# The gather of the next expert and the last transposes set between the slabs of the down product, and each scatter behind the next expert's first feature block

## The reference

```python
def moe_swiglu(h, router, w_gate, w_up, w_down):
    ...
    for e in range(N_EXPERTS):                      # 8 experts, D_FF_EXPERT = 2816
        y = y + gates[:, e:e + 1] * swiglu(hf, w_gate[e], w_up[e], w_down[e])
def swiglu(h, w_gate, w_up, w_down):
    return (jax.nn.silu(h @ w_gate) * (h @ w_up)) @ w_down
```

## Time and profile before

| | |
|---|---|
| median of 3 runs | 2038.96 us (2034.91 to 2041.38) |
| profiled execution: its own time | 2043.77 us |
| profiled execution: span from the first instruction to the last | 2041.9 us |
| mean granted TensorE clock | 0.928 of full speed |
| the eight experts in the loop: first product to the end of the last down product | 997.70 to 1887.99 us |
| the extra round "over", with its gather | about 1896 to 2026 us |

### The profile page before, as it was taken

One profiled execution on the slowest core, in us unless ns is written; L12 is line 12 of the kernel. 1 busy time (PEld: TensorE's weight loads), 2 busy tenths in 40 slices (PEclk: granted clock), 3 DMA queues, 4 the chain that ended last, 5 costly groups with the idle time before them and its releaser, 6 DMA issues.

```text
span 2041.9 us, 23462 instructions
## 1 busy us (share of the span) xinstructions
PE 1838.7 (90%) x8695; PEld 1456.3 (71%) x8696; DVE 1327.3 (65%) x1247; ACT 989.2 (48%) x867; POOL 10.0 (0%) x24
## 2 busy tenths in 40 slices
PE   5899979999999678987799989999899989999786
PEld 2676658888888675556687868878687868777664
DVE  5537464353535647873587868787778869786575
ACT  5443242221221434442566747565666667665463
POOL 0000000000000000000000000000000000000000
PEclk8898979999999789998799989898989999898798
DMA  9535332323222223441498969797889969796593
GB/s 356 185 132 206 124 105 77 107 82 103 86 98 75 80 89 104 145 134 48 144 360 299 350 234 349 291 344 284 293 286 347 331 247 366 282 343 224 186 314 138
DMA packets 215142, 426.25 MB, mean 209 GB/s; under 512 B 8806, under 2 KB 64648, under 8 KB 215052
## 3 DMA queue, kind: packets, MB, share of 16 engines
q1 hardware_dynamic: 210178, 420.33, 58.7%
q10 hardware_dynamic: 4234, 4.57, 0.7%
q0 software_dynamic: 640, 0.04, 0.0%
HBM read 423.86 MB, written 1.05 MB: 208 GB/s over the span
## 4 chain that ended last, share of the span: by engine, by line
PE 74%; DVE 11%; ACT 6%; issue 4%; DMA 3%; SPq 1%; DVEq 0%; ACTq 0%
PE bank L474 22%; PE bank L475 22%; PE bank L476 22%; DVE lo L424 5%; ACT hi L418 4%; PE bank L1781 3%; PE bank L1809 1%; DMA raw<-in_moe_w_up_dram 1%; DMA raw<-in_moe_w_down_dram 1%; PE bank L1481 1%; DMA raw<-in_ada_w_dram 1%; PE bank L1482 1%; DMA raw<-in_moe_w_gate_dram 1%; PE bank L1832 0%; DVE rowmax L1253 0%
## 5 line engine op out<-in xcount | busy, mean ns | idle before, releaser
L424 DVE TENSOR_TENSOR lo<-raw,hi 128x2048 fp32r<-128x2048 f32 x401 | 911.3, 2283 | 350.4 <-ACT hi L418 349.1
L418 ACT ACTIVATE hi<-raw 128x2048 fp32r<-128x2048 f32 x401 | 762.6, 1909 | 524.8 <-PE bank L476 482.9
L474 PE MATMUL bank<-hi,xgh 128*128 128x512 f32 (+1 forms) x864 | 334.0, 387 | 25.9 <-DVE lo L424 25.7
L475 PE MATMUL bank<-lo,xgh 128*128 128x512 f32 (+1 forms) x864 | 328.6, 380 | 0.0
L476 PE MATMUL bank<-hi,xgl 128*128 128x512 f32 (+1 forms) x864 | 328.5, 380 | 0.0
L474 PEld LDWEIGHTS bank<-hi,xgh 128*128 128x128 f32 x864 | 165.5, 192 | 63.2 <-DVE lo L424 27.7
L476 PEld LDWEIGHTS bank<-hi,xgl 128*128 128x128 f32 x864 | 164.9, 191 | 33.6
L475 PEld LDWEIGHTS bank<-lo,xgh 128*128 128x128 f32 x864 | 165.6, 192 | 31.4
L474 PE MATMUL bank<-hi,aTh 128*128 128x512 f32 x396 | 165.4, 418 | 0.9 <-DVE lo L424 0.9
L475 PE MATMUL bank<-lo,aTh 128*128 128x512 f32 x396 | 162.2, 410 | 0.0
L476 PE MATMUL bank<-hi,aTl 128*128 128x512 f32 x396 | 161.9, 409 | 0.0
(11 more groups left out here) (306 smaller groups left out, 2368.0 us busy)
## 6 DMA issues: line engine op xcount, KB each, us to landing
raw<-in_moe_w_gate_dram SPq DMA_DIRECT2D x99, 1024.0 KB, 5.6
raw<-in_moe_w_up_dram SPq DMA_DIRECT2D x99, 1024.0 KB, 5.8
raw<-in_moe_w_down_dram SPq DMA_DIRECT2D x99, 1024.0 KB, 5.2
raw<-in_ada_w_dram SPq DMA_DIRECT2D x48, 1024.0 KB, 5.9
raw<-in_ffn_w_gate_dram SPq DMA_DIRECT2D x11, 1024.0 KB, 5.3
raw<-in_ffn_w_up_dram SPq DMA_DIRECT2D x11, 1024.0 KB, 5.3
raw<-in_ffn_w_down_dram SPq DMA_DIRECT2D x11, 1024.0 KB, 5.8
raw<-in_ab_w_in_dram SPq DMA_DIRECT2D x6, 1024.0 KB, 6.2
```

Of the source, the lines that this page charges most:

```text
L418: nc.scalar.activation(hi[n0 % SPL][:, 0:size], raw[slot][:, 0:size], ACT.Copy).then_inc(hi_ready, 1)
L424: nc.vector.tensor_tensor(lo[n0 % SPL][:, 0:size], raw[slot][:, 0:size], hi[n0 % SPL][:, 0:size].bitcast(F32), ALU.subtract).then_inc(lo_r ...
L474: nc.tensor.matmul(dst, lh, rh, start=first, stop=False, skip_group_check=True)
L475: nc.tensor.matmul(dst, lh, rl, start=False, stop=False, skip_group_check=True)
```

## The change

Four things are done.

1. PE no longer gathers ahead of the down product. The four pieces of the gather follow down slabs j = 0, 1, 3 and 4, the transposes of `Pm` follow j = 5, and the last two transposes (`turn` of block 5) follow j = 2. The pieces have banks of their own (0, 2, 1, 3 and 4), which the feature blocks no longer use then. ACT and DVE read out behind slabs 24 to 30; the `xgl` pieces are now ACT's.
2. The scatter always stands behind block 0 of the *next* expert, in a round or across the loop's edge, and uses four banks, 4 to 7. Its readers `out_hi` and `out_lo` follow slab 2, and `add_out` follows slabs 6 and 7. What belongs to the expert before has `lag`, one loop round back, in its semaphore counts.
3. The first expert has nobody before it. It scatters zeros: two matmuls of zeros fill banks 6 and 7, `PT` is zeroed, and `gate_e` has a column of zeros in front. The last expert's scatter ("tail") follows the loop.
4. In "over" the gather stays whole; the last transposes follow j = 2 there too.

```diff
     def gather(w):
-        return [(("xh", w, 0), 5), (("xh", w, 1), 4), (("xl", w, 0), 5), (("xl", w, 1), 4), (("pt", w), 5)]
+        return [(("xh", w, 0), 0), (("xh", w, 1), 2), (("xl", w, 0), 1), (("xl", w, 1), 3), (("pt", w), 4)]
     def scatter(w):
-        return [(("y", w, o), 5 - o % 2) for o in range(4)]
+        return [(("y", w, o), 4 + o) for o in range(4)]
...
-        return body + between + [(("t", w, 5), 4), (("d", w, 0), 6), (("d", w, 1), 7, (w, 32))]
-    out.append(("first", 1, gather(1)))
-    out.append(("moe", NE // 2, expert(0, [], gather(0)) + expert(1, scatter(0), gather(1)) + scatter(1)))
+        return body + [(("d", w, 0), 6), (("d", w, 1), 7, (w, 32)), (("t", w, 5), 5)] + ahead
+    out.append(("first", 1, [("none", 6), ("none1", 7)] + gather(1)))
+    out.append(("moe", NE // 2, expert(0, scatter(0), gather(0)) + expert(1, scatter(1), gather(1))))
+    out.append(("tail", 1, scatter(1)))
...
@@ ACT, expert @@
             def expert(st, w, it):
                 for s in range(33):
                     split_hi(act, st, (w, s), it=it)
-                    if w == 1 and s == 1:
-                        out_hi(st, 0, it)
+                    if s == 2 and st == "moe":
+                        out_hi(st, 1 - w, it, lag=1 - w)
...
-                    if s == 24:
-                        if st == "moe":
-                            gathered(st, w, it)
-                        act_hi(st, w, 5, it)
+                    if s in (25, 26) and st == "moe":
+                        gathered_hi(st, w, s - 25, it)
+                    if s == 27:
+                        act_hi(st, w, 5, it)
+                    if s in (28, 29) and st == "moe":
+                        gathered_lo(st, w, s - 28, it)
+                    if s == 30 and st == "moe":
+                        gathered_places(st, w, it)
...
@@ DVE, expert @@
             def expert(st, w, it):
                 for s in range(33):
                     splits(st, (w, s), it=it)
-                    if w == 1 and s == 1:
-                        out_lo(st, 0, it)
-                    if w == 1 and s == 5:
-                        add_out(st, 0, it * 2, it)
+                    if s == 2 and st == "moe":
+                        out_lo(st, 1 - w, it, 8 * w, lag=1 - w)
+                    if s in (6, 7) and st == "moe":
+                        add_out(st, w, it * 2 + w, range(2 * s - 12, 2 * s - 10), it)
...
-                    if s == 24:
-                        if st == "moe":
-                            gathered_lo(st, w, it)
-                        act_lo(st, w, 5, it)
+                    if s == 27:
+                        act_lo(st, w, 5, first, it)
...
@@ PE, down_e, behind the products of slab j @@
                     used(ins)
+                    if j == 2:
+                        turn(st, w, 5, it)
+                    if st != "moe":
+                        continue
+                    if j == 0:
+                        pe.wait_ge(p_ready[0], it * 4 + (2 * w + 4))
+                    if j in (0, 1):
+                        gather_rows(st, "xh", w, j, 1 - w, it)
+                    if j in (3, 4):
+                        gather_rows(st, "xl", w, j - 3, 1 - w, it)
+                    if j == 5:
+                        gather_places(st, w, 1 - w, it)
...
@@ PE, expert @@
-                    if w == 1 and c == 0:
-                        scatter(st, 0, it)
+                    if c == 0 and st == "moe":
+                        for h in range(2):
+                            await_emptied(pe, st, ("d", 1 - w, h), it, lag=1 - w)
+                        scatter(st, w, 1 - w, it)
...
-                if st == "moe":
-                    gather(0, st, w, 1 - w, it * 4 + (2 * w + 4), it)
-                turn(st, w, 5, it)
                 down_e(st, w, it)
+            pe.wait_ge(first_zero, 1)
+            for h in range(2):
+                ins = T.matmul(bank(pe, "first", ("none", "none1")[h])[:], ident[:], yM[:, h, 0:512], start=True, stop=True)
+                filled(ins, "first", ("none", "none1")[h])
             gather(0, "first", 1, 0, 2)
```

More of the change, by code:

```diff
@@ L1412, in _ @@
                 expert("moe", 1, it)
-                out_lo("moe", 1, it)
-                add_out("moe", 1, it * 2 + 1, it)
-            for o in (2, 3):
-                await_emptied(dve, "moe", ("y", 1, o), NE // 2 - 1)
+            out_lo("moe", 1, NE // 2 - 1, 16)
+            add_out("tail", 1, NE, range(4), 0)
+            for o in range(4):
+                await_emptied(dve, "tail", ("y", 1, o))
             dve.wait_ge(routed, 1)
@@ L1787, in gather @@
                 filled(ins, stage, ("pt", w))
+            def gather(r, stage, w, par, placed, it=0):
+                pe.wait_ge(p_ready[r], placed)
+                for part in ("xh", "xl"):
+                    for h in range(2):
+                        gather_rows(stage, part, w, h, par, it)
+                gather_places(stage, w, par, it)
             def features(st, kind, w, c, it):
@@ L1831, in scatter @@
                     b = bank(pe, st, ("y", w, o), it)
-                    T.matmul(b[:], PT[:, w, t, :], yeh[:, h, :], start=True, stop=False)
-                    filled(T.matmul(b[:], PT[:, w, t, :], yel[:, h, :], start=False, stop=True), st, ("y", w, o))
+                    T.matmul(b[:], PT[:, places, t, :], yeh[:, h, :], start=True, stop=False)
+                    filled(T.matmul(b[:], PT[:, places, t, :], yel[:, h, :], start=False, stop=True), st, ("y", w, o))
             def expert(st, w, it):
-                for key in (("xl", 1 - w, 1), ("pt", 1 - w)):
-                    if st == "over" or w == 1:
+                if st == "over" or w == 1:
+                    for key in (("xl", 1 - w, 1), ("pt", 1 - w)):
                         await_emptied(pe, st, key, it)
+                else:
+                    for key in (("xl", 1, 1), ("pt", 1)):
+                        await_emptied(pe, st, key, it, lag=1)
                 for c in range(6):
@@ L1855, in _ @@
                 expert("moe", 1, it)
-                scatter("moe", 1, it)
-                for key in (("xl", 1, 1), ("pt", 1)):
-                    await_emptied(pe, "moe", key, it)
+            for h in range(2):
+                await_emptied(pe, "moe", ("d", 1, h), NE // 2 - 1)
+            scatter("tail", 1, 1)
             pe.wait_ge(routed, 1)
@@ L1864, in _ @@
                     expert("over", 0, j)
-                    scatter("over", 0, j)
+                    for h in range(2):
+                        await_emptied(pe, "over", ("d", 0, h), j)
+                    scatter("over", 0, 0, j)
 _INS = ["x", "c", "ctx", "c_ctx", "ada_w", "ada_b", "ab_w_in", "a_v_gain", "a_w_s", "a_b_s", "b_w_pool", "b_scale",
```

114 lines of the change are left out of this document (58 added, 56 removed).

## The result

| | kernel before | changed kernel |
|---|---|---|
| median of the timed runs, us | 2040.17 (2034.91 to 2042.78, 4 runs) | 1957.95 (1954.55 to 1960.86, 4 runs) |
| ratio, 95% interval | | 0.9599 [0.9574, 0.9625] |
| profiled execution: time / span, us | 2043.77 / 2041.9 | 1954.55 / 1952.7 |
| mean granted clock of TensorE | 0.928 | 0.954 |
| loop of eight experts, us | 890.29 | 809.36 |

The change takes 4.0% off, 82.2 us of the medians and 89.2 us between the two profiled executions (that of the changed kernel is the fastest of its four). The page's first part, the answer to the earlier trace rows: PE has 51.6 us less busy time with 12 matmuls more, since fewer of them run at half clock.

A forecast was written before the change was run, and what follows sets the result against it. PE was taken as the bound, losing time to idle waits and half clock. Loop -82.3, zeros +1.6, tail -0.6 and "over" -3.9 sum to -85.2 us; 2038.96 - 85.2 = 1953.8 us, range 1944 to 1982.

The forecast's parts named there:

- The loop: Eight experts at 100.7 us each plus 2.4 us for the first slab: 808.0 us, saving 82.3 us.
- Gather between the slabs: In the down product: no piece waits for a conversion of `aTl`; four pieces of 1.0 us at full clock.
- Scatter behind block 0: In the next expert: the scatter finds everything ready and four free banks, no waits; 1.9 us of matmuls.
- The tight place: Next expert's slab 3: wanted at 8.4 us, ready at 7.9; 0.5 us of room, 0.3 with hand-overs.
- DMA and DVE: In the loop: neither binds; 344 GB/s needed, DVE busy 86.8 us per expert, under 100.7.
- B: In the loop: transfers hold only some 320 GB/s, 59 us more in all, 2013 us; chance 0.06.
- its mild form: In the loop: milder transfer limits, or DVE and ACT slips of 1 to 3 us per expert: 1960 to 1980 us; chance 0.13.
- A: In the down product: the clock falls in part, the saving is 41 us, 1995 us; chance 0.08.
- C: Clock at half for much of the down product: slower, 2199 us with all eleven slabs; chance 0.03.
- The zeros: Ahead of the loop: two fp32 matmuls, 3.4 to 4.1 us, partly inside PE's wait for `Pm`: +1.6 us.
- "over": Behind the loop: down product starts behind block 4's `turn`, without the old waits: -3.9 us, at least -2.
- The tail: Behind the loop: the last scatter no longer waits for banks: -0.6 us.

The follow-up runs named there:

- experiment 1: Changed kernel, but the four gather pieces and the transposes of the places stand in one piece ahead of the down product, new banks kept: 1967.95 us, 0.9656.
- experiment 2: Changed kernel with the gather pieces between the down slabs, but in banks 5, 4, 4, 5, 4, which the transposes use too: 1956.01 us, 0.9593.
- experiment 3: Changed kernel, but the four gather pieces stand in one stretch ahead of the down product, the transposes of `Pm` staying behind slab 5: 1956.4 us, 0.9585.
- experiment 4: Changed kernel, but the scatter of expert w = 1 and its `add_out` go back to the edge of the loop's round: 1975.2 us, 0.9692.
- experiment 5: Changed kernel, but the scatter goes through banks 5 and 4 alone, with all four `add_out` behind slab 5: 1976.12 us, 0.97.
- experiment 6: Changed kernel, but the two fp32 products of zeros ahead of the first gather are shorter fp32r ones: 1958.77 us, 0.9587.
- experiment 7: Changed kernel, but the two fp32 products of zeros move earlier, into PE's wait for the routing: 1956.33 us, 0.9593.
- experiment 8: Changed kernel, but in "over" the last `turn` stands ahead of the down product again, ACT's and DVE's part behind slab 24: 1957.06 us, 0.9585.
- experiment 9: Changed kernel with PE's loop of four rounds written out, the other engines looping as before: 1952.47 us, 0.9564.
- experiment 12: Changed kernel with PE's and ACT's loops written out, and `hi` of three slabs before the gather's read-out at loop start and in "over": 1941.89 us, 0.9514.

## Why the prediction was right

The time, 1957.95 us, lies 4.2 us over the forecast of 1953.8, in the likeliest case.

**The loop** was to take 808.0 us and took 809.36. An expert was 100.7 us and is 100.46. The pieces were 1.0 us and are 0.9; three edges of the round add 2.9 us, for which the sum had no term, since the kernel before hid them under a longer wait. The two errors, 1.9 and 2.9 us, nearly cancel, which is luck.

**Gather between the slabs**, at no wait: as predicted. The prediction gave both reasons, banks and places, and didn't ask whether one would do; experiments 1 to 3 show that either takes the 2.0 us wait away, and that the small matmuls in one stretch keep full clock. From the last feature matmul to the end of the down product an expert took 40.8 to 42.5 us in the kernel before and takes 35.2 in the changed one. That is 54 us of the loop's 81. The waits for bank 4, 2.0 and 0.3 us in each expert, are 19 of them, and the other 35 go with the half clock behind them: 5.1 us as in the earlier trace rows in six experts, some 3.4 in the first two. Experiment 1, with the new banks and the old place, has 41 of the 54 already, and experiment 3, in which nothing waits, has them all. (The kernel before with new banks and nothing else changed was not run.)

**Scatter behind block 0**: as predicted. The tight place was slab 3, wanted at 8.4 us and ready at 7.9. The timeline of DVE and PE in the second expert, whose features begin at 1096.28:

```profile
1100.63 1.28 DVE L1393 TENSOR_TENSOR yel<-bank,yeh 128x512 fp32r<-128x512 f32 x2
1101.83 4.49 DVE L426 TENSOR_TENSOR lo<-raw,hi 128x2048 fp32r<-128x2048 f32 x2
...
1112.44 0.74 DVE L1401 SCALAR_TENSOR_TENSOR X<-bank,gate_e,X 128x512 f32<-128x512 f32 x1
```

```profile
1107.48 0.39 PE L1865 MATMUL bank<-yeh,PT 128*128 128x512 f32 x1
```

The second line holds `lo` of slabs 3 and 4. That of slab 3 is done at 1104.11 and wanted at 1104.68: 0.6 us of room. Slab 8, the other tight one, has 0.8. The scatter's eight matmuls wait for nothing. Experiment 4 puts the price of the old edge at 5.7 us, experiment 5 that of two banks at 2.5 us a scatter.

**DMA and DVE** don't bind: 339 GB/s and DVE busy for 684.70 of 809.36 us. Rivals B and its mild form didn't come. **Rivals A and C**, a clock that falls in the down product, didn't either: 1.00 there. Their case rested on small matmuls and short waits; experiment 3 shows that 32 small ones without a wait leave the clock alone.

**The zeros** were to cost 1.6 us, and the stretch became 1.5 us shorter. The step that failed is "here the clock is half ... two take 3.4 to 4.1 us. They lie in PE's wait": the duration was right (3.76 us in the timeline, of which the gather's first matmul overlaps a part), and so, roughly, was the delay: against the kernel before, the gather's second matmul starts 1.1 us later. But the clock of the gather behind the zeros was taken as unchanged, and there 2.6 us came back (experiments 6 and 7).

**"over"** was to give 3.9 us and gave 3.4, but the step "the down product starts behind block 4's `turn`" isn't the cause: experiment 8 puts the `turn` back and loses nothing. Which of the two other differences named there made the 3.4 us was not tried, so this term is right in size only, by luck. **The tail** gave 0.3 us ahead of "over" and 0.7 behind it, for the 0.6.

With all terms as measured, and without the 2.4 us by which the two executions differ ahead of the change, the saving of the profiled execution is 86.8 us against 85.2 predicted. The medians show 82.2.

The Trainium skill (TensorE: Matmul & The Clock Gate, section Back-to-back issue gap) has 81 ns for a matmul of 128 columns with its weight load; here 16 of them took 1.82 us at full clock in experiment 3, 114 ns each. The measured figure stands.

## What to carry to other kernels

Here a wait of 2 us among matmuls cost more than it showed. Add what the matmuls behind such a wait lose at half clock, and read the windows, not PE's busy share, for it. Before a step is cut up and spread over other work, look at which buffer its waiting instruction wants: here other banks and other places each took the gather's wait away alone. And when a wait is removed, look at what it covered: here an idle time at the loop's edge of 0.6 to 1.4 us, and behind it the conversions that stood in line behind a read-out.

## What the runs showed of the hardware

- Pauses of PE between long matmuls, and whether the clock fell behind them. 0.5 to 1.6 us at the edges of the round: never (30 edges in ten kernels). 1.27 us: never (four cases each in the kernel before and in experiment 5). 1.42 to 1.83 us, waits for `lo` inside "over": once in eleven (1.80 us in experiment 1, while 1.82 and 1.83 us in experiments 7 and 4 left it alone). 2.18 us: in three of four. 3.75 us, at the edges of experiment 4, and 3.5 to 3.6 us at those of the kernel before: in three of three each.
- Pauses with small matmuls. 1.0 us behind 32 of them: in two of eight (experiment 1). 1.9 to 2.0 us among them, in the kernel before: in eight of eight. Between the last transposes of "over": 3.00 us in the kernel before lowered the clock, 2.40 us in experiment 8 didn't.
- So one and the same pause sometimes lowers the clock and sometimes doesn't, and these runs don't show what decides.
- What a fall costs. Between long matmuls about eight of 512 columns follow at half clock, 1.5 to 1.7 us lost. In the gathers of the kernel before, the clock stayed at half for 6 to 10 us.
- A stretch of 32 matmuls of 128 columns, 3.8 us at full clock, doesn't lower the clock while it runs (16 of 16, experiments 1 and 3).
- 3.76 us of fp32 products, begun at half clock, brought the clock up within the 16 small matmuls behind them; with a wait of 2.48 us between, the gather ran at half clock (3.64 and 3.62 us).
- At the edge of the round of a loop on PE there was an idle time of 0.5 to 1.6 us that no semaphore explains. The same code written out, 3,872 matmuls, had none (experiments 9 and 12).
